# Conditioning sums of eight later column groups: transposed in blocks and folded by VectorE before one product, and taken out of their bank earlier

## What is computed

```
mod = silu(c) @ w_ada + b_ada              # 2048 -> 6*2048: shift, scale, gate, twice
hn = rms_norm(h) * (1 + sc1) + sh1
proj = hn @ w_in                           # 5664 columns: attention q, k, v; DeltaNet q, k, v, z, b, a
mixed = concat(attention(...), gated_deltanet(...)) @ w_out      # 8 + 8 heads of 128
h = h + gt1 * mixed
hn = rms_norm(h) * (1 + sc2) + sh2
u_gate, u_val = split(dwconv(hn @ w_up) + b_ffn_conv)
h = h + gt2 * ((silu(u_gate) * u_val) @ w_down)
out = rms_norm(h) * final_norm
```

## Time and profile before

| | |
|---|---|
| median of 3 runs | 2612.41 us (2611.73 to 2614.58) |
| the profiled execution | 2611.63 us, span 2610.0 us |
| TensorE busy | 2517.7 us, 96% of the span |
| VectorE, ScalarE, GpSimd busy | 1477.6, 903.4, 201.7 us |
| mean granted TensorE clock | 0.985 |
| chain that ended last | PE 89%, DVE 6%, issue 2% |
| `ada_sums`, L1510 | 128 passes of TensorE, 14.7 us busy |
| a head in the loop | some 97.5 us from one L1837 to the next |

### The profile page before, as it was taken

One profiled execution on the slowest core, in us unless ns is written; L12 is line 12 of the kernel. 1 busy time (PEld: TensorE's weight loads), 2 busy tenths in 40 slices (PEclk: granted clock), 3 DMA queues, 4 the chain that ended last, 5 costly groups with the idle time before them and its releaser, 6 DMA issues.

```text
span 2610.0 us, 34653 instructions
## 1 busy us (share of the span) xinstructions
PE 2517.7 (96%) x11920; PEld 2060.3 (79%) x11920; DVE 1477.6 (57%) x1917; ACT 903.4 (35%) x1274; POOL 201.7 (8%) x278
## 2 busy tenths in 40 slices
PE   4999999999999899989999999999999999999997
PEld 4777787787787678868888888888888888888786
DVE  6837678678678584474444444444444444444454
ACT  4334424424424334342222222222222222222344
POOL 3401121111121021000000000000000000000000
PEclk7999999999999899999999999999999999999998
DMA  9933454454454355323333333323333333333233
GB/s 353 324 109 113 131 161 128 133 158 130 135 157 129 109 145 153 97 73 98 96 96 88 104 97 96 96 88 98 104 96 97 96 89 96 100 96 96 87 95 130
DMA packets 431728, 318.20 MB, mean 122 GB/s; under 512 B 12950, under 2 KB 403905, under 8 KB 431169
## 3 DMA queue, kind: packets, MB, share of 16 engines
q1 hardware_dynamic: 401712, 212.19, 28.2%
q0 software_dynamic: 29184, 104.87, 12.4%
q10 hardware_dynamic: 785, 0.51, 0.1%
HBM read 313.33 MB, written 4.19 MB: 122 GB/s over the span
## 4 chain that ended last, share of the span: by engine, by line
PE 89%; DVE 6%; issue 2%; ACT 1%; DMA 1%; POOL 0%; DVEq 0%; ACTq 0%; POOLq 0%
PE pw L1474 23%; PE pw L1476 22%; PE pw L1475 22%; PE pw L1458 2%; PE pw L1460 2%; PE pw L1459 2%; PE pd L1791 2%; PE pd L1768 1%; PE pd L1783 1%; DMA ka<-in_w_ada_dram 1%; DVE w_lo L969 1%; PE pd L1731 1%; PE pd L1808 1%; PE pd L1803 1%; DVE ada_acc L985 1%
## 5 line engine op out<-in xcount | busy, mean ns | idle before, releaser
L1474 PE MATMUL pw<-act_hi,w_hi 128*128 128x512 f32 x1984 | 793.8, 400 | 3.8 <-DVE w_lo L969 3.0
L969 DVE TENSOR_TENSOR w_lo<-raw,w_hi 128x1024 fp32r<-128x1024 f32 x426 | 524.0, 1230 | 481.4 <-ACT w_hi L573 475.0
L1476 PE MATMUL pw<-act_hi,w_lo 128*128 128x512 f32 x1984 | 774.3, 390 | 0.0
L1475 PE MATMUL pw<-act_lo,w_hi 128*128 128x512 f32 x1984 | 773.1, 390 | 0.0
L573 ACT ACTIVATE w_hi<-raw 128x1024 fp32r<-128x1024 f32 x426 | 450.2, 1057 | 542.9 <-PE pw L1476 444.6
L1474 PEld LDWEIGHTS pw<-act_hi,w_hi 128*128 128x128 f32 x1984 | 373.2, 188 | 90.2 <-issue 16.4
L1475 PEld LDWEIGHTS pw<-act_lo,w_hi 128*128 128x128 f32 x1984 | 373.2, 188 | 81.4 <-issue 6.9
L1476 PEld LDWEIGHTS pw<-act_hi,w_lo 128*128 128x128 f32 x1984 | 372.8, 188 | 78.8
L1474 PE MATMUL pw<-mh_hi,w_hi 128*128 128x512 f32 x704 | 276.1, 392 | 3.0 <-DVE w_lo L969 3.0
L1476 PE MATMUL pw<-mh_hi,w_lo 128*128 128x512 f32 x704 | 274.2, 389 | 0.0
L1475 PE MATMUL pw<-mh_lo,w_hi 128*128 128x512 f32 x704 | 274.0, 389 | 0.0
(11 more groups left out here) (291 smaller groups left out, 2469.8 us busy)
## 6 DMA issues: line engine op xcount, KB each, us to landing
raw<-in_w_up_dram SPq DMA_DIRECT2D x172, 512.0 KB, 4.0
ada_w<-in_w_ada_dram POOLq DMA_DIRECT2D x128, 512.0 KB, 4.6
raw<-in_w_in_dram SPq DMA_DIRECT2D x84, 512.0 KB, 3.9
raw<-in_w_down_dram SPq DMA_DIRECT2D x64, 384.0 KB, 3.4
raw<-in_w_down_dram SPq DMA_DIRECT2D x64, 320.0 KB, 3.2
raw<-in_w_out_dram SPq DMA_DIRECT2D x32, 512.0 KB, 4.6
DD<-in_w_ada_dram POOLq DMA_DIRECT2D x9, 512.0 KB, 8.0
EG<-in_w_ada_dram POOLq DMA_DIRECT2D x9, 512.0 KB, 6.7
```

What stands on the lines that cost most here:

```text
L969: V.tensor_tensor(w_lo[slot][:], raw[slot][:], w_hi[slot][:].bitcast(F32), ALU.subtract).then_inc(lo_made.sem, 1)
L1474: M(bank, w_hi[slot][:, k, :], hi[:, k0 + k, :], start=first, stop=False)
L1475: M(bank, w_hi[slot][:, k, :], lo[:, k0 + k, :], start=False, stop=False)
L1476: ins = M(bank, w_lo[slot][:, k, :], hi[:, k0 + k, :], start=False, stop=last)
```

## The change

VectorE gets two instructions at the end of each head, after the last `ada_one`: a transpose of `ada_acc` in blocks of 32 x 32 into 128 x 1024 elements of `XW` (the storage of `XT` and `WZ`, now one tile), and a sum over groups of 32 neighbours, which leaves 128 x 32 values in `qr`'s storage. TensorE then makes one product with a constant stationary operand of 128 x 128 (ones where row and column agree modulo 32) and those 32 columns, in place of the eight. The sum lies in another layout in its bank, so `ada_columns` takes it out with four instructions of 32 partitions in place of one of 128, and it is moved: from behind `s(1)` to behind `s(0)`, ahead of convolution 1. The constants grow by 128 columns, and the semaphore counts are adapted.

```diff
-C_N = C_PAR + 2 * LEVELS
+C_FOLD = C_PAR + 2 * LEVELS
+C_N = C_FOLD + P
...
+    c[:, C_FOLD:C_FOLD + P] = p % 32 == f % 32
...
             def ada_columns(h):
                 dve.wait_ge(*ada_sum.after(h))
-                V.tensor_tensor(at(mod, h + 4, 8), pd[5][:, 0:8], at(col, h + 4, 8), ALU.add).then_inc(ada_out.sem, 1)
+                for q in range(4):
+                    r = slice(32 * q, 32 * q + 32)
+                    V.tensor_tensor(at(mod[r], h + 4, 8), pd[5][r, q:32:4], at(col[r], h + 4, 8), ALU.add).then_inc(ada_out.sem, 1)
...
                     if part == 0:
                         s(0)
+                        if not first:
+                            ada_columns(h - 1)
...
                 s(1)
-                if not first:
-                    ada_columns(h - 1)
                 ada_next(0)
...
                     ada_next(12 + c)
+                dve.wait_ge(*ada_step.after(h, KT))
+                V.transpose(ada_blocks, ada_acc[:]).then_inc(ada_step.sem, 1)
+                dve.wait_ge(*ada_step.after(h, KT + 1))
+                V.tensor_reduce(ada_groups, ada_blocks.rearrange("p (c s) -> p c s", s=32), AX.X, ALU.add).then_inc(ada_step.sem, 1)
                 dve.wait_ge(*onorm.after(h))
...
             def ada_sums(h):
                 pe.wait_ge(*ada_step.after(h))
-                for i in range(8):
-                    ins = M(pd[5][:, i:i + 1], ada_acc[:, i * P:(i + 1) * P], ones[:, 0:1], start=True, stop=True)
-                ins.then_inc(ada_sum.sem, 1)
+                M(pd[5][:, 0:32], cst[:, C_FOLD:C_FOLD + P], ada_groups, start=True, stop=True).then_inc(ada_sum.sem, 1)
```

More of the change, by code:

```diff
@@ L167, in build @@
         PTb = sb("PTb", [P, 4, NB, P], F32, mixer)
-        XT = sb("XT", [P, NB, P], F32, mixer)
-        WZ = sb("WZ", [P, 2, NB, P // 2], F32, mixer)
+        XW = sb("XW", [P, 2, NB, P], F32, mixer)
+        XT, WZ = XW[:, 0], XW[:, 1].rearrange("p b (a n) -> p (b a) n", a=2).rearrange("p (a b) n -> p a b n", a=2)
         Wc, Zc = WZ[:, 0], WZ[:, 1]
@@ L181, in build @@
         EGf = EG[:].rearrange("p d n -> p (d n)")
-        ktf, vtf, XTf, Wf, Zf = one(ktok[:]), one(vtok[:]), one(XT[:]), one(Wc), one(Zc)
+        ktf, vtf, XTf, Wf, Zf = one(ktok[:]), one(vtok[:]), one(XT), one(Wc), one(Zc)
         tmpf = tmp[:].rearrange("p d n -> p (d n)")
@@ L199, in build @@
         qr = qr_t[:]
+        ada_blocks, ada_groups = two(XW[:]), qr_t[:, 0:32]
         prob = [tmp[:, 0, :], tmp[:, 1, :]]
@@ L305, in build @@
         first_sum, first_out = signal("first_sum"), signal("first_out")
-        ada_step = signal("ada_step", KT)
+        ada_step = signal("ada_step", KT + 2)
         ada_sum = signal("ada_sum")
-        ada_out = signal("ada_out")
+        ada_out = signal("ada_out", 4)
         block = ctx.enter_context(nc.Block())
@@ L519, in ada_load @@
                 if not (first and k < 2):
-                    pool.wait_ge(ada_step.sem, h * KT + k - 1)
+                    pool.wait_ge(ada_step.sem, h * (KT + 2) + k - (3 if k < 2 else 1))
                 pool.dma_start(ada_w[k % 2][:], A["w_ada"][0, k * P:(k + 1) * P, bass.ds((4 + h) * ADA_W, ADA_W)]) \
@@ L1002, in ada_one @@
                 else:
-                    dve.wait_ge(ada_step.sem, KT * h + k)
+                    dve.wait_ge(ada_step.sem, (KT + 2) * h + k)
                     V.scalar_tensor_tensor(ada_acc[:], w, cond[:, k:k + 1], ada_acc[:], ALU.mult, ALU.add).then_inc(ada_step.sem, 1)
@@ L1222, in head @@
                 dve.wait_ge(*lower_made.after(h))
-                V.tensor_tensor(WZ[:].rearrange("p a b n -> p (a b n)").rearrange("p (b n) -> p b n", n=P), CT,
+                V.tensor_tensor(WZ.rearrange("p a b n -> p (a b n)").rearrange("p (b n) -> p b n", n=P), CT,
                                 lvl[:, 0].unsqueeze(1).broadcast_to([P, NB, P]), ALU.mult).then_inc(lt_masked.sem, 1)
@@ L1226, in head @@
                 dve.wait_ge(*rope_step.after(h))
-                V.transpose(XTf, WZ[:].rearrange("p a b n -> p (a b n)")).then_inc(lt_turned.sem, 1)
+                V.transpose(XTf, WZ.rearrange("p a b n -> p (a b n)")).then_inc(lt_turned.sem, 1)
                 dve.wait_ge(*lt_turned.after(h))
@@ L1230, in head @@
                 for d in range(2):
-                    V.scalar_tensor_tensor(T_of[d], XT[:], cst[:, C_PAR + d:C_PAR + d + 1], eye, ALU.mult, ALU.add) \
+                    V.scalar_tensor_tensor(T_of[d], XT, cst[:, C_PAR + d:C_PAR + d + 1], eye, ALU.mult, ALU.add) \
                         .then_inc(t_first.sem, 1)
@@ L1308, in _ @@
             low_halves(1)
-            dve.wait_ge(ada_out.sem, ADA_LATER)
+            dve.wait_ge(ada_out.sem, 4 * ADA_LATER)
             V.tensor_scalar(mod[:, 64:80], mod[:, 64:80], 1.0, None, ALU.add).then_inc(scale2_made.sem, 1)
```

## The result

| | median (lowest to highest), us | before in the same runs | ratio, 95% interval |
|---|---|---|---|
| changed kernel | 2620.10 (2619.24 to 2622.04), 7 runs | 2613.14, 7 runs | 1.0028 (1.0018 to 1.0037) |
| changed kernel, measured again with the last experiments | 2618.50 (2616.91 to 2621.46), 11 runs | 2613.53, 15 runs | 1.0021 (1.0011 to 1.0030) |

The change costs 5 to 7 us, where 2.1 us were forecast, and neither interval contains 1. The forecast was 2614.5 us in a range that ended at 2619.5: the first measurement lies above the range, the second at its upper end. Further down, one execution of the kernel before took 7961.88 us and one of e7 6565.68 us; the ratios are made without such slow ones.

The account below looks back on a forecast made before the run. VectorE's and ScalarE's chain bounds a loop head. Terms: +1.26 us for heads 1 to 6, +0.64 for head 7, +0.19 for constants, together +2.1: 2613.7, or 2614.5 us for the median; range 2610.0 to 2619.5.

Parts of the forecast that it names:

- What bounds a head: Loop heads, L1837 to L1731: the chain is VectorE's and ScalarE's; only 0.45 us before L1172 are TensorE's to give.
- The wait for the low half: Sign on TensorE: a wait for the low half of `s(0)` before `run(8, 14)`, 0.7 us in each loop head.
- TensorE's passes, transpose and group sum: 14 passes less per head save 1.49 us; transposes 1.41 and reductions 1.30 us at the head's end cost nothing.
- 4 x 0.16 = 0.64 us: Cost of the four `ada_columns` in front of convolution 1, each at its whole duration without the address computation.
- 6 x 0.64 - 2.58: Heads 1 to 6: chain 0.64 us later each, less 2.58 us of L1172's waits for L1714: +1.26 us.
- The 0.45 us in front of L1172: VectorE's wait for TensorE's L1714 in head 3, the most that TensorE's saving could remove from the chain there.
- The 0.64 us of head 7: Head 7: low halves of the mixer's output, made behind convolutions 1 and 2, reach TensorE later: +0.64 us.
- The 0.19 us for the constants: Loading 64 KiB more constants in the first slices costs +0.19 us at most, taken in full.
- Dearer small instructions: Rival: the four `ada_columns` at 0.35 us each, 7.4 us more, 2619.8 us; chance 0.05.
- The clock: Rival: longer TensorE idleness brings one half-clock window of 1.7 us lost per loop head, 2624.7 us; chance 0.06.
- The cover at the head's end: Rival: transpose and group sum outlast VectorE's idleness before L1296; one microsecond over gives 2621.5 us; chance 0.03.
- the saving: Rival: TensorE's 1.49 us comes off each of the six loop heads, 8.9 us, 2603.5 us; chance 0.07.

Follow-up runs that it names:

- e7: Kernel before with the cosine product moved early into another buffer, ahead of the wait for ScalarE: 2607.14 us, ratio 0.9979.
- e3: Changed kernel, each of the four column instructions on all 128 partitions and 2 columns instead of 32 partitions and 8: 2615.96 us, ratio 1.0009.
- e2: Changed kernel with the four column instructions moved from in front of convolution 1 to behind convolution 2: 2613.23 us, ratio 1.0004.
- e5: Changed kernel with the four column instructions behind `s(1)`, where the single one stood: 2615.70 us, ratio 1.0013.
- e1: Kernel before with only the 128 further columns of constants: 2613.42 us, ratio 1.0004.
- e9: Changed kernel, the four column instructions each in its own quarter of the partitions, but with 2 columns instead of 8: 2619.17 us.
- e4: Kernel before, eight products kept, columns taken out by four instructions of 32 partitions in front of convolution 1: 2617.42 us, ratio 1.0018.
- e11: Changed kernel with columns behind convolution 2, cosine product early, and block 0's score maximum in front of a transpose: 2600.97 us, ratio 0.9956.
- e10: As e9, but all four column instructions on the first quarter, partitions 0 to 31: 2613.16 us.

## Why the prediction was wrong

**What bounds a head: right.** The chain through VectorE and ScalarE is what counts. 0.50 us off it gave 3.04 us over six heads (e3), 0.77 gave 4.71 (e2), and 1.5 us less of TensorE's work in each gave 0.6 in all six (e2 against before). Most of the signs came as listed: the product of the sums 0.14 us to the next, L1177 without a wait, the wait in front of L1738 longer, L1305 released by ScalarE after 2.82 us of idleness. The wait for the low half stands in the row with 0.18 us where I had 0.7, but the row shows only a part of it: from L1693 to `run(8, 14)` it is 2.14 us, in the earlier trace rows 1.40, so 0.74 more. Wrong were the spacing of the four, 0.19 for 0.16, and the head's length, 0.74 us more where I had 0.2.

**TensorE's passes, transpose and group sum: right.** 1.56 us less for 1.49, and 1.25 + 1.22 us for 1.41 + 1.30, hidden. The 0.4 us that the prediction adds for two waits stand in no row: from the transpose's start to the group sum's end it is 2.49 us.

**The term that was mis-sized:** "4 x 0.16 = 0.64 us" measured 0.77, and 0.76 at L732's start. 0.16 is the duration of one alone; held one behind another they come 0.19 apart. This is 0.12 to 0.13 us a head, under 1 us in all.

**The step that failed:** "6 x 0.64 - 2.58", with its ground that "from 517.27 VectorE works without a pause to L1184". A row without a wait in brackets isn't a row of plain work. The credit arrived where I had put it: L1177 is later by 0.22 us, the prediction has 0.64 - 0.43 = 0.21. That the two agree so well is luck, for it measured 0.75 - 0.53, both terms larger by 0.1. And the credit was gone one instruction later, since L1178 ends 0.55 us behind GpSimd's mask product, and L1175 releases that one, which the four instructions delay whole. The 0.45 us in front of L1172 were never TensorE's alone to give: they covered a hold of the same size. So a head loses 0.75 - 0.53 + 0.52 = 0.74 us, and six lose 4.4; measured 4.1 and 4.5 from the two profiles (before had one head of 97.84 us among five of 97.5). The sum had 1.26. I read VectorE, ScalarE and TensorE through head 3, and not GpSimd, whose two rows would have shown it; L1173 took 0.74 us even there, where the same instruction takes 0.68 once it starts behind the mask product (e5).

**Head 7 and the load.** The 0.64 us of head 7 show at the product that waits for the mixer's low halves: it starts 18.17 us behind the head's L1844 (907.48, with L1844 at 889.31), before 17.39, so 0.78 later. At the head's end they can't be told: head 7 as a whole was 112.15 and 113.90 us against 112.19, and its stretches of half clock are 17.1 and 20.5 us in all against 13.7 before. The 0.19 us for the constants don't show in e1.

**The range.** Its upper end doesn't follow from its own terms: 2617.1 with 2.2 us of spread and 1.7 us for one more window of half clock is 2621.0, not 2619.5. With that end the first measurement would have been inside, and so would the rival at 2619.8. It would not have mended the step above: the loss in the heads was 4.1 to 4.5 us for 1.26.

**The rivals.** Dearer small instructions gave 2619.8, near the result, but for 0.35 us each, and they measured 0.19: the number fits, the reason doesn't. The clock did not fall within the heads, with waits of 0.80 and 1.03 us in each. The row of the six heads (columns as above, the granted clock is the 1.00):

```profile
299.70:889.00 589.30, 574.22 (x3024) 457.11 (x3023) 467.92 (x696) 238.29 (x414) 96.69 (x131) 1.00 0.47 139
```

The cover at the head's end was long enough, and the saving did not arrive.

**Open.** The heads in the loop explain 4.1 to 4.5 of the 5 to 7 us. In the first profile 1.5 us more lie ahead of head 1, in the second 0.9; among all fourteen profiles that part goes from 296.4 to 299.8 us, and what moves it was not looked for. A further 2.1 us of the first profile lie behind head 7, with the stretch of half clock of 10.2 us where the repetition has 6.8 us (the windows above), as the kernel before has. Among the ten profiles with the new sum the longer stretch is in four (the changed kernel, e3, e5, e9), among the four without it (before, e1, e4, e7) in none. That is too few to say whether the change makes it more frequent, and it wasn't tried by itself.

## What to carry to other kernels

Before crediting a wait that a change removes, ask of each instruction behind it what the next releaser is, on all engines, GpSimd too: a wait can cover a hold of the same length, and here a row that is 0.05 us longer than it is without the hold was its only sign on VectorE. A small instruction put into the chain costs its spacing there and not its duration, so put it where the chain has passed on to another engine (behind convolution 2, where ScalarE has what it needs next, the same four cost nothing that can be told). And where a chain on one engine bounds the loop, its own order is the first thing to look at: the cosine product moved ahead and one maximum moved in front of a transpose (e2 to e11) gave 12 us, where 112 passes taken from the busiest engine (before to e2) gave none that can be told.

## What the runs showed of the hardware that was not expected

- Four VectorE instructions of 32 x 8 or 32 x 2 take 0.77 or 0.75 us to the start of the next when each starts in another quarter of the partitions (changed kernel, e9). Four of 32 x 2 in one quarter (e10), or of 128 x 2 (e3), take 0.27 us.
- A VectorE instruction of 128 x 512 with two SBUF operands that starts during GpSimd's mask product of 1.16 us ends 0.54 to 0.56 us after it: 1.28 us for the cosine product, 1.06 to 1.08 for the addition, where each takes 0.68 or 0.69 if it starts later (e5, e7). With one operand in a bank it takes 0.68 us beside the mask product.
- A reduction of 128 x 1024 to 32 values a partition takes 1.22 us, no more than the transpose of the same size, 1.25 us, and both together cost the kernel nothing that can be told (e2).
- The same wait of TensorE, 2.98 us for a low half ahead of the heads (the product behind it starts at 201.91 in the kernel before, at 203.97 in e1), was followed by 3.4 us at a granted clock of 0.50 in one profile and by none in the other. The kernel before, then e1 (columns as above, the clock behind the five engines):

```profile
202.90:206.30 3.40, 3.40 (x10) 2.62 (x9) 3.33 (x6) 2.07 (x4) 0.00 (x0) 0.50 0.56 154
```

```profile
204.00:212.00 8.00, 8.00 (x32) 5.96 (x33) 7.79 (x12) 4.82 (x8) 0.00 (x0) 1.00 0.47 131
```
